# A two-layer encoder trunk on one core: the first layer's opening in another order, and VectorE's split last in the loop

## What is computed

```python
xn = rms_norm(x, norm_mix[layer])
proj = xn @ w_in[layer]        # 1024 x 4096: q, k, v, u and 2048 gate columns
q = rotary(q, positions)
k = rotary(k, positions)
a = diff_attention(q, k, v, lam)              # 4 heads, two softmaxes each
a = rms_norm(a, attn_subln[layer]) * (1.0 - lam_init)
s = s5_bidirectional(u, lam_re, lam_im, log_dt, b_re, b_im, c_re, c_im, d_skip)
s = gelu(s); s = s * sigmoid(s @ w_glu[layer])
merged = gates[0] * (a @ w_branch[layer, 0]) + gates[1] * (s @ w_branch[layer, 1])
x = x + merged @ w_out[layer]
```

## Time and profile before

| | |
|---|---|
| median of 3 runs | 1395.47 us (1391.1, 1395.47, 1395.57) |
| profiled execution, its own time | 1390.18 us |
| its span | 1388.4 us |
| TensorE busy | 1350.3 us, 97% |
| VectorE busy | 1107.1 us, 80% |
| ScalarE busy | 897.8 us, 65% |
| GpSimd busy | 332.5 us, 24% |
| mean granted clock of TensorE | 0.995 |

### The profile page before, as it was taken

How to read it: one execution, slowest core, us unless ns; L and a number is a source line. 1 busy time by engine, 2 the same in 40 slices (tenths; PEclk the granted TensorE clock), 3 DMA queues, 4 the chain that set the end, 5 groups by cost and what they waited for, 6 DMA issues and landing times.

```text
span 1388.4 us, 22394 instructions
## 1 busy us (share of the span) xinstructions
PE 1350.3 (97%) x7982; PEld 1108.9 (80%) x7982; DVE 1107.1 (80%) x1013; ACT 897.8 (65%) x915; POOL 332.5 (24%) x425
## 2 busy tenths in 40 slices
PE   8889999999999999999999999999999999999996
PEld 6678787888888787878888888888888888888885
DVE  6988678555565686788888889888888888898886
ACT  6366745444454566457777777777777777777775
POOL 7958419994000384010000000000000000000100
PEclk9999999999999999999999999999999999999998
DMA  8342355655645432979999999999999999999991
GB/s 330 122 127 104 137 171 193 197 182 186 198 145 173 132 123 99 351 264 339 369 374 377 386 366 377 391 362 387 379 375 388 368 375 390 352 391 350 386 347 31
DMA packets 194574, 385.12 MB, mean 277 GB/s; under 512 B 17616, under 2 KB 56912, under 8 KB 194384
## 3 DMA queue, kind: packets, MB, share of 16 engines
q1 hardware_dynamic: 189392, 369.99, 74.0%
q0 software_dynamic: 3360, 12.06, 2.9%
q10 hardware_dynamic: 1760, 2.23, 0.5%
HBM read 375.85 MB, written 7.34 MB: 276 GB/s over the span
## 4 chain that ended last, share of the span: by engine, by line
PE 86%; DVE 6%; ACT 3%; issue 2%; DMA 1%; SPq 1%; POOL 1%; ACTq 0%; POOLq 0%; DVEq 0%
PE bank L698 80%; DVE lo L1747 3%; ACT hi L1303 1%; PE bank L1197 1%; PE bank L716 1%; PE bank L842 1%; DMA raw<-in_w_in_dram 1%; PE bank L867 1%; PE bank L954 0%; PE bank L1180 0%; POOL raw L2346 0%; PE bank L1071 0%; ACT raw L1353 0%; ACT at_hi L1654 0%; PE bank L824 0%
## 5 line engine op out<-in xcount | busy, mean ns | idle before, releaser
L1747 DVE TENSOR_TENSOR lo<-raw,hi 128x2048 fp32r<-128x2048 f32 x344 | 801.7, 2342 | 153.7 <-ACT hi L1303 153.0
L1303 ACT ACTIVATE hi<-raw 128x2048 fp32r<-128x2048 f32 x344 | 658.0, 1916 | 186.3 <-PE bank L698 183.6
L698 PE MATMUL bank<-hi,at_hi 128*128 128x512 f32 x1288 | 513.5, 399 | 14.3 <-DVE lo L1747 3.4
L698 PE MATMUL bank<-hi,at_lo 128*128 128x512 f32 x1288 | 503.6, 391 | 0.0
L698 PE MATMUL bank<-lo,at_hi 128*128 128x512 f32 x1288 | 502.8, 391 | 0.1
L698 PEld LDWEIGHTS bank<-hi,at_hi 128*128 128x128 f32 x1288 | 242.7, 188 | 68.6 <-issue 7.6
L698 PEld LDWEIGHTS bank<-hi,at_lo 128*128 128x128 f32 x1288 | 242.5, 188 | 52.3
L698 PEld LDWEIGHTS bank<-lo,at_hi 128*128 128x128 f32 x1288 | 242.8, 189 | 47.9 <-DVE lo L1762 0.5
L698 PE MATMUL bank<-hi,ht_hi 128*128 128x512 f32 x432 | 168.8, 391 | 0.9 <-DVE ht_lo L2212 0.9
L698 PE MATMUL bank<-hi,ht_lo 128*128 128x512 f32 x432 | 168.2, 389 | 0.0
L698 PE MATMUL bank<-lo,ht_hi 128*128 128x512 f32 x432 | 168.1, 389 | 0.0
(11 more groups left out here) (312 smaller groups left out, 1172.5 us busy)
## 6 DMA issues: line engine op xcount, KB each, us to landing
raw<-in_moe_w_dram SPq DMA_DIRECT2D x528, 512.0 KB, 6.7
raw<-in_ffn_w_dram SPq DMA_DIRECT2D x66, 512.0 KB, 4.4
raw<-in_w_in_dram SPq DMA_DIRECT2D x64, 512.0 KB, 4.6
raw<-in_w_branch_dram SPq DMA_DIRECT2D x16, 512.0 KB, 4.4
raw<-in_w_out_dram SPq DMA_DIRECT2D x16, 512.0 KB, 4.8
raw<-in_w_glu_dram SPq DMA_DIRECT2D x4, 512.0 KB, 4.3
moe_sum<-xres POOLq DMA_DIRECT2D x3, 512.0 KB, 6.0
qk<-in_x_cols_dram SPq DMA_DIRECT2D x2, 512.0 KB, 6.2
```

The costliest lines, as they stand in the source:

```text
L698: return pe.matmul(o, a, b, start=start, stop=stop)
L1303: act.activation(hi[:, slot, :], src, ACT.Copy).then_inc(hi_ready, 1)
L1747: tt(lo[:, slot, :], src, hi[:, slot, :].bitcast(f32), SUB).then_inc(lo_ready, 1)
```

## The change

What it does, by engine.

SP: x_rows goes from behind tile 0 to behind tile 2; B goes behind tile 3, C and the constants behind tile 4, the lambda vectors and subln behind tile 6, after waits for par_ready and for lo of all of x (they now lie where the first parameters and gains were). HALVED becomes (0, 1, 2, 3). d_skip comes from the host as ready diagonals, one transfer of 128 KB per layer (layer 1 on GpSimd's queue), and inner_diagonal with its semaphore goes.

TensorE: first_projs takes four tiles by halves; v is summed in TR[0] and TR[1] and not in PJ, so tile 4 waits for u's evacuation alone; tiles 4 and 5 go ahead of the transposes of u.

ScalarE: hi of x for k = 4 to 7 in place of VectorE (which takes k = 2 and 3); the exponential behind tile 0, the sine behind tile 1, the squares behind tile 2, then tile 3, the root and tile 4; u's evacuation, B and C, tile 5, v out of TR, tiles 6 and 7 ahead of u's transposed evacuation.

VectorE: tiles 1, 2 and 3 by halves, then the inverse roots; in the mixer two factors, split 4, two factors, power 0 in two halves with splits 5 and 6 between, rotary of q, split 7, powers 1 to 4, rotary of k, splits 8 and 9, and the lambda sums behind them. In the loop of both layers the order is row_max(s), rotated(s + 1), softmax_factors(s), scanned(s + 1), weights(s), split of tile s + 10; the factor on subln goes behind the loop.

The diff, cut:

```diff
-        HALVED = (0, 1, 3)
+        HALVED = (0, 1, 2, 3)
...
                         if t == 1:
-                            sp.dma_start(xres[:, :, :].rearrange("p t d -> p (t d)"), x_rows).then_inc(x_in, 16)
                             sp.dma_start(x_flat[:, 1024:2048], x_cols[:, 1024:2048]).then_inc(cols_second, 16)
                         if t == 3:
+                            sp.dma_start(xres[:, :, :].rearrange("p t d -> p (t d)"), x_rows).then_inc(x_in, 16)
+                        if t == 4:
                             sp.dma_start(braw_flat, ssm_b[0, :, :]).then_inc(b_in[0], 16)
+                        if t == 5:
                             for r in range(2):
                                 sp.dma_start(craw[r].rearrange("p q d h -> p (q d h)"), ssm_c[0, r, :, :]).then_inc(c_in[0], 16)
+                            sp.dma_start(cst[:, C_ID:C_ID + P], consts[:, C_ID:C_ID + P]).then_inc(ident_in, 16)
                             sp.dma_start(cst[:, C_TRI:C_END], consts[:, C_TRI:C_END]).then_inc(loads, 16)
+                        if t == 7:
+                            sp.dma_start(kdiag.rearrange("p q h -> p (q h)"), ssm_d[0, :, :]).then_inc(kdiag_in[0], 16)
+                            sp.wait_ge(par_ready, 1)
+                            sp.wait_ge(x_lo, KD)
+                            sp.dma_start(lam_rows, attn_lambda.rearrange("l a c -> (l a c)").partition_broadcast(P)).then_inc(lam_in, 16)
...
-                    elif first and i > 0:
-                        pe.wait_ge(pj_free[th], pj_read(l, i - 1))
+                        pe.wait_ge(pj_free[th], pj_read(l, 0 if (l, i) == (0, 2) else i - 1))
...
+            def first_projs():
+                for t, half in ((t, half) for t in range(4) for half in range(2)):
+                    s, k0, odd = t % SPLITS, 4 * (t % 2), t % 2
+                    for th in range(TH):
+                        o = (PJ if t < 2 else TR)[th][:, :]
+                        rows = [(k0 + k, slice(th * P, (th + 1) * P), slice(k * 512, (k + 1) * 512)) for k in (2 * half, 2 * half + 1)]
...
-                pe.wait_ge(kdiag_ready, l + 1)
+                pe.wait_ge(kdiag_in[l], 16)
...
                 if l == 0:
+                    proj(t + 4, l, 2, 0, True, False)
+                    proj(t + 5, l, 2, 4, False, True)
                     pe.wait_ge(ident_in, 16)
+                    for th in range(TH):
+                        pe.wait_ge(pj_free[th], pj_read(l, 1))
...
+                    x_hi((0, 1))
+                    split_half(0, 0)
+                    split_half(0, 1)
                     act.wait_ge(lr_ready, 1)
                     act.activation(row(R_er), row(R_lr), ACT.Exp)
+                    act.wait_ge(cols_second, 16)
+                    x_hi(range(4, KD))
+                    split_half(1, 0)
+                    split_half(1, 1)
                     act.wait_ge(angle_ready, 1)
                     act.activation(par[:, SIN, :], row(R_red), ACT.Sin)
                     act.activation(row(R_sh), row(R_red), ACT.Sin, scale=0.5).then_inc(act_par, 1)
+                    split_half(2, 0)
+                    split_half(2, 1)
                     act.wait_ge(x_in, 16)
                     squares(0)
                     squares(1)
+                    split_half(3, 0)
+                    split_half(3, 1)
...
                     dve.wait_ge(par_ready, 1)
+                    for k in range(2):
+                        next_factor(k)
+                    split_static(t + 4)
+                    for k in range(2, 4):
+                        next_factor(k)
                     dve.wait_ge(braw_full, 2)
+                    input_power([(0, 8, [bbar[:, r, 0:8] for r in range(2)])], 0, 0, 8)
+                    split_static(t + 5)
+                    input_power([(8, PAIRS, [bbar[:, r, 8:PAIRS] for r in range(2)])], 0, 8, PAIRS)
+                    split_static(t + 6)
+                    dve.wait_ge(loads, 16)
+                    rotary(l, "q", qk[:, 0, :, :])
+                    split_static(t + 7)
+                    dve.wait_ge(states_first, 2)
+                    for k in range(1, 5):
+                        input_power(b_power(k), k)
+                    dve.memset(dve_mark, 0.0).then_inc(b_part, 1)
+                    dve.memset(power_mark, 0.0).then_inc(b_ready, 1)
+                    rotary(l, "k", qk[:, 1, :, :])
+                    split_static(t + 8)
+                    split_static(t + 9)
...
-                    if s in LOOP_PROJ[l] and s < 7:
-                        split_static(loop_proj(l, s)[0] + 2)
+                    if s < 7:
+                        rotated(l, s + 1)
                     softmax_factors(l, s)
                     if s < 7:
-                        rotated(l, s + 1)
+                        scanned(l, s + 1)
                     weights(l, s)
                     if s < 7:
-                        scanned(l, s + 1)
+                        split_static(loop_proj(l, s)[0] + 2)
...
+            for k in range(2, 4):
+                ts(at_hi[:, k, :], x_t[:, k, :], gain_cols[:, k:k + 1], None, MUL).then_inc(x_hi_dve, 1)
...
             split_half(1, 0)
             split_half(1, 1)
+            split_half(2, 0)
+            split_half(2, 1)
             variances(0)
-            split_static(2)
-            inverse_roots(0)
             split_half(3, 0)
             split_half(3, 1)
-            dve.wait_ge(loads, 16)
+            inverse_roots(0)
             mixer(0)
```

## The result

The changed kernel takes **1380.82 us** (median, 1380.31 to 1380.97), the kernel before 1393.76 beside it (1391.1 to 1395.57): ratio 0.9912, 95% interval 0.9892 to 0.9933. The profiled execution took 1380.81 (span 1379.0) against 1390.18 (span 1388.4), a gain of **9.4 us** where my sum said 5.9. The other 5.3 us of the error (1389.6 - 1380.8 = 8.8 = 3.5 + 5.3) come from the median that I subtracted from.

What follows compares the result with a forecast made beforehand. TensorE, busy 97% of the span, was taken to bound the kernel, with VectorE's row setting inner()'s start. 4.8 - 0.9 + 2.0 = 5.9 us off the median 1395.47 gave 1389.6 us, range 1384 to 1395.

Steps and rivals of the forecast that it cites:

- my sum: Whole kernel: 4.8 for an earlier inner(), less 0.9 for the clock, plus 2.0 in the loop, 5.9 us gained.
- The base: Whole kernel: profiled execution of before lies 5.3 us below the median, so the 1384.3 forecast becomes 1389.6 against the median.
- inner()'s start: First layer before the loop: VectorE finishes power 4 at 64.0, inner() starts at 64.2 against 68.98, 4.8 us earlier.
- Rival B: Front: VectorE's long row starts no earlier, at 27.6 again; gain 2.6 us, 1392.9; chance 0.14.
- The three covers: Before inner(): ScalarE's hi ready for VectorE's splits, tiles 4 and 5 done for q's rotary, GpSimd's c_ready by 63.3.
- The clock: inner(): TensorE's idle time of over 9 us ahead of it lowers the clock, costing 0.9 us, bounds 0 and 1.6.
- rival D: Between inner() and the loop: clock stays low after the long idle; 4.2 us slower, 1399.7; chance 0.07.
- The loop: Last turns of both layers: VectorE's later split closes TensorE's spots of 1.21 and 0.90 us; 2.0 gained, bounds 0 and 2.1.
- rival C: Loop gives nothing: GpSimd's turn with the split beside it ends after 156; gain 3.9 us, 1391.6; chance 0.12.
- At the other turns nothing is won: Loop turns other than the last: no gain, since TensorE was full, 39.00 of 39.00 us between 105 and 144.
- Rival E: Front: less contention than now, par_ready at 22.5; gain 8 us, 1387.5; chance 0.05.
- The chance for faster by over 0.3%: Whole kernel: 0.62 for faster by more than 4.2 us, 0.31 for within that, 0.07 for slower.

Runs made afterwards that it cites:

- before_filled: Kernel before plus four spare matmuls of 448 columns in TensorE's idle spot of tile 1; twelve runs gave 1389.61 to 1391.77 us.
- front_only: Changed kernel with the old order in the loops of both layers; 1384.73 us, ratio 0.9933.
- after_late: Changed kernel plus four spare matmuls between the two halves of tile 1; 1383.02 us.
- kept_warm: Changed kernel plus nine spare matmuls in TensorE's idle spot ahead of inner(); median 1381.42 us.
- power_twice: Changed kernel with power 1 of the decay computed a second time on VectorE; median 1385.33 us.
- rows_early: Changed kernel with x_rows asked for right behind tile 0 again, as in the kernel before; median 1382.83 us.
- before_again: Kernel before, no edit, run again; eight runs gave 1389.8 to 1392.4 us and four 1396.0 to 1397.0.
- loop_only: Kernel before with only VectorE's order in the loop changed to the new one; 1388.49 us, ratio 0.9954.

## Why the prediction was right in kind and wrong in size

**The base: wrong, 5.3 of the 8.8 us.** I worked out 1384.3 from the profiled execution and then moved it up by 5.3, because the runs of before lay that much above it. That treats the spread as a constant that goes with any kernel. It belongs to the idle spot at 17.31, which before_filled takes away without moving the early group; the changed kernel has no such spot, and no late group: of the 29 runs below 1390 of the six kernels with its front and its banks (the changed one, front_only, after_late, kept_warm, power_twice, rows_early) none lies over 1.7 us from another of the same kernel. Moreover two of the three runs that I had were of the late group, which over 73 runs is 31. I had the pieces on the page: this spot was the one after which the trace showed full clock, and I quoted it as a counter-example to the rule about an idle array. It was one draw of several: full clock (before), half clock at once (before_again), half clock after 1.2 us (loop_only). The rule of the Trainium skill that I cited there ("TensorE: Matmul & The Clock Gate", section on the HAM clock gate: an idle array drops to 1.2 GHz) agrees with before_again, 0.50 behind an idle 3.61 us, and not with the first profile, 1.00 behind 3.35.

**inner()'s start, 4.8 predicted, 5.60 measured.** The start of the row was right: 24.23 against 24.4 as summed (3.43 earlier, not 3.3), released by GpSimd's par as said; so were its bounds, and rows_early shows that it hangs on the sine. Rival B is out. The time of the sine, 14.4 in the sum and 14.54 measured, was luck in part: I had it follow from ScalarE's list, which had reached it by 13.85; it then waited 0.68 us for GpSimd's angle, whose last two operations had stretched to 1.40 and 1.09 us beside a split. The lambda sums are out of the row (1.1), and with inner_diagonal gone VectorE's last instruction is 0.16 us ahead of TensorE, not 0.98 (0.82). The halves of power 0 cost 0.6, not 0.4: two of 2.2 us against 3.85 for the whole. What failed is that I took the rest of the row at its old length: it is 0.85 shorter (3.43 + 1.10 + 0.82 - 0.60 leave that much to 5.60). The two timelines show where it sits. From start to start the splits of tiles 4, 5 and 6 take 2.34, 2.25 and 2.42 us and not 2.49, 2.73 and 2.75 (0.96 less together), the four factors 3.84 and not 4.00, the rotary of q and the split of tile 7 together 0.26 more. GpSimd's large products begin at 36.43 now and at 32.74 before, so the splits of tiles 4 and 5 now lie ahead of them; that this is the reason is argued from two traces, not isolated. The three covers held: no wait in the row, no idle time from 9.11 to 55.09, c_ready at 60.77. The mark came at 63.22, not 64.0, and power_twice shows that the row's end sets inner().

**The clock, -0.9 predicted, +0.54 measured.** That the idle spot of over 9 us (8.29) would be followed by clock 0.50 was right, and it lasts 3.7 us or so. The step that failed is the price: I took a half of what such a stretch costs in the splitting stage, where TensorE is full, though I had seen the hole of 1.33 us in inner() and said that it may take up a part. It took up all of it: inner() took 7.82 us before, 4.93 of them busy; it takes 7.3 now with half of them at half clock, and 7.64 in kept_warm at full. With it rival D is out: the clock was back before the next work.

**The loop, 2.0 predicted within 0 and 2.1, 3.25 measured** (2.05, 0.92 and 0.28). The two spots closed, 1.21 and 0.90, as worked out; rival C is out, though GpSimd's operation does take 3.3 us with the split beside it in every turn. "At the other turns nothing is won" is the step that failed: I had looked at 105 to 144, where TensorE is full, and not at the turn ahead of it, 94.90 to 105.03, which took 10.13 us and was busy for 9.76; it lost 0.76 (9.37 now), 0.3 ahead of the transposes of the weights, which wait for VectorE, and 0.4 ahead of s5_out(1). The last 0.3 lie behind the loop of layer 1; no row of mine says where.

**Together** 0.8 + 1.44 + 1.25 = 3.5 over the sum. Rival E (more, 0.05) was the nearest in time, for another reason than I gave it: par_ready was not earlier. The chance for faster by over 0.3% stood on the right side. The range was too narrow at its lower end since it did not go below the sum taken from the profiled execution.

## What to carry to other kernels

When the runs of a kernel spread in two groups, look for what in the trace can come out two ways, and ask whether the change removes it, before you subtract from the median. Price a slow clock by what the stretch is limited by: dense large matmuls pay for it, small ones with holes that nobody releases did not here. And a part of a change that lets a bank be emptied later (u behind hi of tile 4) may live only by another part that makes the next work use other banks (the turning banks); look for such pairs before you price either.

## What the runs showed of the hardware

- Behind the same idle spot in the same kernel, TensorE's granted clock was 1.00 in one execution (3.35 us idle) and 0.50 in another (3.61 us idle); in loop_only, with the same spot (3.62 us idle), it was 1.00 for 1.2 us and then 0.51. Filled with four spare matmuls, the runs lay within 2.2 us in place of 8.8 beside them.
- VectorE's operations of 32 to 64 elements took 0.18 to 0.47 us beside small work of GpSimd; beside its products of 128x512 most took 0.95 to 1.33 us and the rest 0.18 to 0.22. The same sixteen operations took 4.0, 3.6, 8.9 or 11.7 us as they started at 27.66, 29.34, 30.62 or 32.17, with the products beginning at 32.5 to 32.8.
- A chain of 273 small matmuls took 7.6 to 7.8 us at full clock, with 2.8 to 2.9 us of holes in it, and 7.3 us with half of it at clock 0.50.
